# Prompt rows of eight experts fetched and turned together, the first expert's turn in two banks, the rotation of the first attention on GpSimd

## The reference

```
def apply_rope(x, cos, sin):
    x1, x2 = jnp.split(xf, 2, axis=-1)
    return jnp.concatenate([x1 * cos - x2 * sin, x2 * cos + x1 * sin], axis=-1)

def expert_choice_ffn(h, w_router, w_gate, w_up, w_down):      # 16 experts
    cap = EC_CAPACITY * T // N_EXPERTS                         # 128 sample rows, 16 prompt rows
    aff = jax.nn.softmax(jnp.einsum('btd,de->bte', h, w_router), axis=-1)
    gate, idx = lax.top_k(aff.swapaxes(1, 2), cap)
    xg = jax.vmap(lambda hb, ib: hb[ib])(h, idx)
    y = einsum(silu(xg @ w_gate) * (xg @ w_up), w_down) * gate
    return zeros.at[idx].add(y)                                # per group
```

## Time and profile before

| | us |
|---|---|
| median of three timed runs | 4399.0 (4393.88 to 4404.57) |
| profiled execution | 4391.62 |
| its span | 4389.8 |
| TensorE busy | 3666.0 (84%) |
| VectorE busy | 2445.7 (56%) |
| ScalarE busy | 1652.6 (38%) |
| GpSimd busy | 601.4 (14%) |
| mean granted clock of TensorE | 0.904 of full speed |

### The profile page before, as it was taken

One profiled execution on the slowest core, in us unless ns is written; L12 is line 12 of the kernel. 1 busy time (PEld: TensorE's weight loads), 2 busy tenths in 40 slices (PEclk: granted clock), 3 DMA queues, 4 the chain that ended last, 5 costly groups with the idle time before them and its releaser, 6 DMA issues. The chain is left out here.

```text
span 4389.8 us, 55873 instructions
## 1 busy us (share of the span) xinstructions
PE 3666.0 (84%) x22188; PEld 2687.1 (61%) x22188; DVE 2445.7 (56%) x3797; ACT 1652.6 (38%) x2480; POOL 601.4 (14%) x457
## 2 busy tenths in 40 slices
PE   3997869797839999999599978419996579999995
PEld 2994524343726666666499956319995446666663
DVE  3234341233477888887412454445555668888884
ACT  2114520000215555555211156524433145555653
POOL 2001110110100101000300000015651010101000
PEclk7998879898969999999699998759997789999997
DMA  4218521411536787777344120343325348777875
GB/s 157 89 60 280 170 72 72 162 53 50 174 141 237 282 294 277 271 278 281 109 118 114 63 92 13 108 145 80 99 55 197 134 160 293 283 270 273 291 283 193
DMA packets 363736, 743.38 MB, mean 169 GB/s; under 512 B 98888, under 2 KB 204247, under 8 KB 362376
## 3 DMA queue, kind: packets, MB, share of 16 engines
q1 hardware_dynamic: 343818, 683.00, 44.1%
q0 software_dynamic: 17040, 56.40, 5.1%
q10 hardware_dynamic: 2618, 0.40, 0.1%
HBM read 634.25 MB, written 106.10 MB: 169 GB/s over the span
## 5 line engine op out<-in xcount | busy, mean ns | idle before, releaser
L2023 DVE TENSOR_TENSOR moe_w_low<-ffn_w,moe_w_high 128x1024 fp32r<-128x1024 f32 x768 | 912.9, 1221 | 132.6 <-ACT moe_w_high L1956 116.5
L1956 ACT ACTIVATE moe_w_high<-ffn_w 128x1024 fp32r<-128x1024 f32 x768 | 785.7, 1055 | 436.1 <-DMA ffn_w<-moe_w_gate 144.0
L1886 PE MATMUL moe_small<-ffn_w,moe_xT 128*16 128x512 f32 x2048 | 238.3, 594 | 0.0
L1983 DVE TENSOR_SCALAR moe_xT<-moe_turn,keep_coef 128x128 f32<-128x128 f32 (+1 forms) x512 | 142.0, 344 | 116.7 <-PE moe_turn L1842 116.7
L1866 PE MATMUL moe_G<-moe_w_high,moe_xT_high 128*128 128x512 f32 x512 | 179.8, 433 | 16.1 <-issue 16.1
L297 PE MATMUL proj_mm<-proj_hT_low,proj_w_high 128*128 128x384 f32 x576 | 193.2, 335 | 0.0
L297 PE MATMUL proj_mm<-proj_hT_high,proj_w_low 128*128 128x384 f32 x576 | 193.1, 335 | 0.0
L297 PE MATMUL proj_mm<-proj_hT_high,proj_w_high 128*128 128x384 f32 x576 | 193.1, 335 | 0.0
L297 PE MATMUL proj_mm<-proj_w_high,proj_hT_low 128*128 128x416 f32 (+1 forms) x504 | 176.5, 350 | 0.0
L297 PE MATMUL proj_mm<-proj_w_high,proj_hT_high 128*128 128x416 f32 (+1 forms) x504 | 176.1, 349 | 0.0
L2547 PE MATMUL gdnc_a<-gdnc_T,gdnc_kg 128*128 128x64 f32 (+1 forms) x864 | 102.1, 267 | 88.3 <-ACT gdnc_T L2597 86.1
(11 more groups left out here) (450 smaller groups left out, 7555.5 us busy)
## 6 DMA issues: line engine op xcount, KB each, us to landing
ffn_w<-moe_w_gate SPq DMA_DIRECT2D x256, 512.0 KB, 7.0
ffn_w<-moe_w_up SPq DMA_DIRECT2D x256, 512.0 KB, 7.8
ffn_w<-moe_w_down SPq DMA_DIRECT2D x256, 512.0 KB, 5.9
attnrun_m_w<-w_ada SPq DMA_DIRECT2D x40, 1024.0 KB, 10.8
scratch_conv<-proj_zf POOLq DMA_DIRECT2D x24, 512.0 KB, 2.9
scratch_tm<-proj_tm SPq DMA_DIRECT2D x45, 208.0 KB, 2.0
proj_w_raw<-even_w_in SPq DMA_DIRECT2D x24, 384.0 KB, 3.9
scratch_spec<-filt_res SPq DMA_DIRECT2D x36, 256.0 KB, 2.2
```

Of the source, the lines that this page charges most:

```text
L1886: nc.tensor.matmul(out, stat, w, start=k == 0, stop=k == KD - 1, tile_position=(0, 32 * q)).then_inc(small_done, 1)
L1956: nc.scalar.activation(w_high[n % CUT_ROOM][:], raw_rows(wall, n), ACT.Copy).then_inc(w_up, 1)
L1983: ins = nc.vector.tensor_scalar(xT[e % 2][:, k, cols], turned(k)[:, cols], co[:, 0, k:k + 1], co[:, 1, k:k + 1], ALU.mult, ALU.add)
L2023: nc.vector.tensor_tensor(w_low[n % CUT_ROOM][:], raw_rows(wall, n), w_high[n % CUT_ROOM][:].bitcast(F32), ALU.subtract).then_inc(w_cut, 1)
```

## The change

Three things are changed. In `experts` the row numbers of the prompt slots go to memory and come back as one column of 128 for every eight experts; two indirect DMAs fetch all prompt rows of the layer, and four groups of four turns fill `xpT`, behind k = 0 to 3 of expert 0. An expert's sample rows are turned in two groups of four, behind k = 4 and 6 of the expert before; for expert 0 the second group goes to a bank of Y. `xT` has one buffer. The places of evictions, rounding and cutting move with them, and expert 0's small matmuls of k 0 to 3 all stand behind k = 5. The row of the prompt's gate is loaded as four pieces. In the attention of layer 0 the rotations of tiles 2 to 8 run on GpSimd, two ahead of each bias addition.

```diff
+        def rope(eng, ops, n):        # the body of VectorE's rope(n), on the engine given
...
             for n in order[:ready[0] + 1]:
                 if even and n < NT:
-                    rope(n)
+                    rope(dve, nc.vector, n)
...
-                if even and p % 4 == 1 and p // 4 in steady:
-                    rope(steady[p // 4])
...
+            turning = list(steady.values()) if even else []
+            if even:
+                pool.wait_ge(trig_in, 32)
-            for g in range(MG):
+            for g in range(max(MG, -(-len(turning) // 2))):
+                for n in turning[2 * g:2 * g + 2]:
+                    rope(pool, nc.gpsimd, n)
                 if g == 0:
                     pool.wait_ge(m_bias_in, 64)
...
-        fills = (range(0, 3), range(3, 6), range(6, KD))
+        NF = 2
+        def turned(k, e=1):
+            return (Y[:, 0, :] if e == 0 and k >= 4 else turn_bank)[:, (k % 4) * P:(k % 4 + 1) * P]
...
-            for c in range(2):
-                sp.dma_start(rowg[:, c, :], all_rows(io["mrow"][l, c, 5 * D:6 * D])).then_inc(row_in, 16)
+            sp.dma_start(rowg[:], all_rows(io["mrow"][l, 0, 5 * D:6 * D])).then_inc(row_in, 16)
+            for q in range(4):
+                src = io["mrow"][l, 1, 5 * D + 256 * q:5 * D + 256 * (q + 1)]
+                sp.dma_start(rowgp[32 * q:32 * (q + 1), :], all_rows(src, 32)).then_inc(row_in, 16)
...
+            def fetch_prompts():
+                pool.dma_start(io["prompt_rows"].rearrange("e r -> r e"), keep.slot_p[0:CAP_P, :].bitcast(F32),
+                               allow_slow_non_contiguous=True).then_inc(rows_out, 16)
+                pool.wait_ge(rows_out, 16)
+                pool.dma_start(rows_p[:].bitcast(F32), io["prompt_rows"].rearrange("(g j) r -> (j r) g", j=PG),
+                               allow_slow_non_contiguous=True).then_inc(rows_in, 16)
+                pool.wait_ge(rows_in, 16)
+                for g in range(E // PG):
+                    nc.gpsimd.indirect_dma_start(out=xgp[g][:], out_offset=None, in_=io["xn"],
+                                                 in_offset=bass.IndirectOffsetOnAxis(ap=rows_p[:, g:g + 1], axis=0)).then_inc(xgp_in, 16)
...
             fetch(0)
             fetch(1)
+            fetch_prompts()
...
-                for k in fills[i]:
-                    nc.tensor.transpose(turned(k)[:, 0:CAP_S], xg[e % 2][:, k * P:(k + 1) * P], keep.ident[:])
-                    mm = nc.tensor.transpose(turned(k)[:, CAP_S:SLOTS], xgp[e % 2][:, k * P:(k + 1) * P], keep.ident[0:CAP_P, 0:CAP_P])
+                for k in range(4 * i, 4 * i + 4):
+                    mm = nc.tensor.transpose(turned(k, e), xg[e % 2][:, k * P:(k + 1) * P], keep.ident[:])
+            def turn_prompts(n):
+                g, i = divmod(n, 2)
+                if n == 0:
+                    pe.wait_ge(xgp_in, 16 * (E // PG))
+                    pe.wait_ge(x_set, NF)
+                else:
+                    pe.wait_ge(xp_set, n)
+                for k in range(4 * i, 4 * i + 4):
+                    mm = nc.tensor.transpose(turned(k), xgp[g][:, k * P:(k + 1) * P], keep.ident[:])
+                mm.then_inc(xp_turned, 1)
...
-                    if e + 1 < E and k in (3, 5, 7):
-                        turn_tokens(e + 1, (k - 3) // 2)
-                    if k in (3, 5):
-                        small_rows(e, range(k - 3, k - 1), False)
+                    if e == 0 and k < 4:
+                        turn_prompts(k)
+                    if e + 1 < E and k in (4, 6):
+                        turn_tokens(e + 1, (k - 4) // 2)
+                    if k == 3 and e:
+                        small_rows(e, range(0, 2), False)
+                    if k == 5:
+                        small_rows(e, range(2 if e else 0, 4), False)
...
-                if (e, m, k) == (1, "u", 0):
+                if (e, m, k) == (1, "g", 1):
                     round_tokens(1)
-                if m == "d" and k == 3 and e + 2 < E:
+                if m == "d" and k == 1 and e + 2 < E:
                     round_tokens(e + 2)
...
-                if m == "g" and e + 1 < E and k in (5, 7):
-                    set_tokens(e + 1, (k - 5) // 2)
+                if e == 0 and m == "g" and 2 <= k < 6:
+                    set_prompts(k - 2)
+                if m == "g" and e + 1 < E and k == 6:
+                    set_tokens(e + 1, 0)
                 if (e, m, k) == (1, "g", 0):
-                    set_tokens(1, NF - 1)
-                if (e, m, k) == (1, "g", 1):
+                    set_tokens(1, 1)
+                if (e, m, k) == (1, "u", 1):
                     cut_tokens(1)
+                if m == "d" and k == 0 and e + 2 < E:
+                    set_tokens(e + 2, 1)
                 if m == "d" and k == 2 and e + 2 < E:
-                    set_tokens(e + 2, NF - 1)
-                if m == "d" and k == 3 and e + 2 < E:
                     cut_tokens(e + 2)
```

More of the change, by code:

```diff
@@ L784, in spread_sums @@
             mm.then_inc(spread_mm, 1)
+        def rope(eng, ops, n):
+            eng.wait_ge(tok_in[n], 16)
+            x = tok[:, n, 0:640].rearrange("p (h a d) -> p h a d", a=2, d=32)
+            q_out = tok[:, n, 0:512].rearrange("p (j s a d) -> p s j a d", s=2, a=2, d=32)
+            trig, c1, s1 = m["trig"], m["c1"], m["s1"]
+            if n:
+                eng.wait_ge(roped, n)
+            if n < NTS:
+                cos, sin = (trig[:, i, n:n + 1, :].unsqueeze(1).broadcast_to([P, 10, 2, 32]) for i in range(2))
+                ops.tensor_tensor(c1[:], x, cos, ALU.mult).then_inc(chain, 1)
+                ops.tensor_tensor(s1[:], x, sin, ALU.mult).then_inc(chain, 1)
+                eng.wait_ge(chain, 2 * n + 2)
+                for a, op in ((0, ALU.subtract), (1, ALU.add)):
+                    ops.tensor_tensor(x[:, 8:10, a, :], c1[:, 8:10, a, :], s1[:, 8:10, 1 - a, :], op)
+                    ins = ops.tensor_tensor(q_out[:, :, :, a, :], c1[:, 0:8, a, :].rearrange("p (s j) d -> p s j d", s=2),
+                                            s1[:, 0:8, 1 - a, :].rearrange("p (s j) d -> p s j d", s=2), op)
+            else:
+                ops.tensor_copy(c1[:], x).then_inc(chain, 1)
+                eng.wait_ge(chain, 2 * n + 1)
+                for a in range(2):
+                    ins = ops.tensor_copy(q_out[:, :, :, a, :], c1[:, 0:8, a, :].rearrange("p (s j) d -> p s j d", s=2))
+            ins.then_inc(roped, 1)
         @blk.tensor
@@ L875, in take_outputs @@
                 nc.vector.tensor_tensor(oT[:, g % 2], po[:], spread[:], ALU.mult).then_inc(o_done, 1)
[L877 to L898, removed]
             def take_keys(n):
@@ L1763, in experts @@
         xg = [s.sb(f"xg{i}", [P, D]) for i in range(2)]
-        xgp = [s.sb(f"xgp{i}", [CAP_P, D]) for i in range(2)]
-        xT = [s.sb(f"xT{i}", [P, KD, SLOTS]) for i in range(2)]
+        PG = P // CAP_P
+        rows_p = s.sb("rows_p", [P, E // PG], U32)
+        xgp = [s.sb(f"xgp{i}", [P, D]) for i in range(E // PG)]
+        xpT = s.sb("xpT", [P, KD, E // PG, P])
+        xT = s.sb("xT", [P, KD, CAP_S])
         xT_high, xT_low = ([s.sb(f"xT_{n}{i}", [P, KD, CAP_S], F32R) for i in range(2)] for n in ("high", "low"))
@@ L1774, in experts @@
         yp = [s.sb(f"yp{i}", [CAP_P, D]) for i in range(2)]
-        rowg = s.sb("rowg", [P, 2, D])
+        rowg = s.sb("rowg", [P, D])
+        rowgp = s.sb("rowgp", [P, 256])
         G, U, Y = (s.ps(n, [P, 2, BANK]) for n in "GUY")
@@ L1831, in turn_tokens @@
             def turn_tokens(e, i):
-                if i:
+                if e and i:
                     pe.wait_ge(x_set, NF * e + i)
-                else:
-                    pe.wait_ge(xg_in[e % 2], 32 * (e // 2 + 1))
+                elif i == 0:
+                    pe.wait_ge(xg_in[e % 2], 16 * (e // 2 + 1))
                     if e >= 2:
@@ L1870, in small_rows @@
             def small_rows(e, ks, down):
-                if not down and ks[0] == 0 and e >= 2:
-                    pe.wait_ge(yp_done, e - 1)
+                if not down and ks[0] == 0:
+                    pe.wait_ge(xp_set, 4)
+                    if e >= 2:
+                        pe.wait_ge(yp_done, e - 1)
                 if down and ks[0] == 0:
```

45 lines of the change are left out of this document (26 added, 19 removed).

## The result

The changed kernel takes 4346.0 us (median of 4 runs, 4344.0 to 4347.6) against 4396.4 (4 runs, 4393.1 to 4404.6): ratio 0.988, 95% interval 0.9865 to 0.990. The forecast was 4330, its range 4312 to 4358. It is faster, by 50 us and not by 69. The two profiled executions differ by 47.0 (spans 4389.8 and 4342.8).

The account below looks back on a forecast made before the run. TensorE's issue was taken as the bound. Gains and losses of 58 + 11 - 0.4 - 3.4 + 3.8 = 69 us gave 4322.6 off the profiled 4391.6, 4330 off the median 4399; range 4312 to 4358 with the nearer half of (a) and (b).

Parts of the forecast that it names:

- main case: Whole kernel: forecast of 4330 us off the median, spanning 4314 to 4343 by its bounds; chance 0.78 together with (d).
- part 1: Token turns of experts 1 to 15: 2.08 us saved a loop, 58 us over 28 loops; bounds 28 x 1.0 to 28 x 2.5.
- Part 2: First expert's start: TensorE starts 5.5 us earlier a layer, 11 us for two layers; bounds 8 to 13.
- Part 3: Prompt rows through GpSimd's queue: 4.7 us for each slot-number DMA, TensorE waits 0.2 us a layer; bounds nothing to 15.
- Part 4: Rest of loop 0: takes 41.2 us, 1.7 more than before, costing 3.4 us over two layers; bounds 0 to 8.
- Part 5: First attention's rotations moved from VectorE to GpSimd: TensorE waits of 3.8 us go; bounds 0 and 7.
- (a): Rival on the turns: 16-row turns only fill free slots or weights come late, 28 x 1.0 saved, 4360; chance 0.11.
- (d): Rival in attention: GpSimd late for the keys, 5 us lost replace 3.8 gained, 4339; chance 0.78 together with the main case.
- (b): Rival on prompt rows: each slot-number DMA takes 12.3 us, 2 x 15 us of waiting plus half-clock restarts, 4363; chance 0.08.
- (c): Rival in expert loops: VectorE blocked on turned tokens, later cuts slip, 76 us lost instead of 58 gained, 4464; chance 0.03.
- the 48 that would have refuted the forecast: Sign of being wrong in the expert loops: the period stays above 48 us an expert; 47.1 was forecast.
- this sign of being wrong: Sign at the first expert's start: prompt rows land later than 1310 us.

Follow-up runs that it names:

- a1: The changed kernel with rows_p allocated last, no longer amid the expert stage's tiles: 4335.4 us, ratio to the kernel before 0.986.
- b1: The kernel before with an unused 8-byte tile between xg and xgp, moving later expert-stage tiles by 32 bytes: 4417.8 us, ratio 1.0046.
- a5: a1 with both token-turn groups directly ahead of the small matmuls (k = 3 and 5, not 4 and 6) for experts 1 to 14: 4336.3 us.
- c1: a1 plus a5's turns, reordered loop 0 end, earlier small matmuls, later gate-row wait, earlier slot numbers, split prompt-fetch semaphores, early Silu load: 4310.6 us.

## Why the prediction was right in kind and 19 us off in size

- *The range*: the main case with its bounds was given as 4314 to 4343, and 4346 lies outside it. The result is inside 4312 to 4358 only because half of two rivals was added. The 4343 doesn't follow from the bounds either: part 1 at its own lower bound, 28 for 58, would by itself give 4360.
- *What bounds the kernel*: right. TensorE stands at 100 of 100 in the steady stretch, before and after; VectorE's slack and the weight transfers held, as costed.
- *Part 1, the mis-sized term*: 2.08 us a loop were forecast, 58 in all, and 1.39 x 28 = 39 came (the table's 37.7 also holds the last loops, which turn nothing and pay the shift). Of the missing 0.69, 0.51 (14 us) is the shifted tiles, shown by a1 and by b1 in the other kernel. The working priced what the diff issues and took for granted that the untouched pairs keep their 0.4545; the declaration of `rows_p` in the diff changed those. The other 0.18 (5 us): aligned, the period is 47.30. I priced the turns by their start-to-start cost and the entries by the entry alone, but the k step behind any interruption runs 0.03 or so slower as a whole (pairs of 0.46 to 0.47), and the old order had two k steps with no interruption ahead of them. That part is read from timelines; a5, which restores those two steps, gives back 0.12.
- *Part 2*: right. 5.3 and 5.7 us a layer against 5.5; first G matmul 13.8 us after the fetch against 14.
- *Part 3*: the value chosen failed, the bounds held. It was 4.7 us for each of the two DMAs; the write took 8.0 to 9.6 in all kernels that write 4-byte pieces, the reading back 2.5 to 2.9. The wait is 1.0 and 2.95 us, not 0.2. By the Trainium skill ("DMA: Bandwidth & Descriptors", "Anatomy of one DMA", some 2.0 us plus bytes) there would, as an estimate, have been no wait: the reading back is near that, the write isn't.
- *Part 4*: the new stall was called at some 5 us and is 5.41 and 4.83. Still the loop is longer than the 41.2 us forecast (the terms listed add up to 41.4): 43.2 and 44.1. Parts 3 and 4 together cost 9.3 where 3.8 were forecast; 4.0 of it are the waits for prompt rows, which leaves 5.3 for part 4 by itself, inside its bounds of 0 to 8. Of these 5.3 the stall is 1.4 more than before, weights called "about even" are 1.3, and some 3 (an estimate, half of 16.0 - 9.8 us) are time at clock 0.50, for which the working had 0.3 a layer. The matmuls themselves take some 0.5 less, with at most 1.1 for the 96 shifted pairs in it.
- *Part 5*: right in sign and in the waits that it named; it left out the clock. The rotation takes 5.1 us on GpSimd as forecast, and the three waits of 1.18, 1.24 and 1.37 us are gone. The stage is 7.3 shorter, just above the bound of 7: 3.8 of waits, and 6.8 us less at clock 0.50 (23.9 before, 17.1 after), worth some 3.4 as an estimate. In five of nine executions this second part did not come, or half of it did. The Trainium skill ("Perfetto Trace Analysis", "Optimizing Scalar/DVE Operations") says that such a move might not help, for the shared read port; read as a gain of 0, that did not hold here.
- *Rivals*: (a), half the turns' price at 4360, is 14 us from the result where the forecast is 16, but by luck: its mechanism, 16-row turns that fill free slots, did not hold, for aligned the turns save 1.89 a loop. (d), 4339, is nearest of all in number, and what it describes didn't occur: the attention gained. Of (b) the write is late, at 8.0 to 9.6 us and not 12.3, and the reading is early; the wait is 1 to 3 us and not 15. (c) did not occur.
- *Signs*: the turns, TensorE at 100 of 100, the first G matmul, the stall and the rotations came as called; VectorE's longest sum of the rotation now takes 0.42 us and not 2.26. The period, at 47.8, is short of the 48 that would have refuted the forecast. The wait for prompt rows was to be under 1 us and is 1.03 and 2.95. They were not to land later than 1310, which is 20.5 us behind the first fetch: TensorE goes on with them after 20.3 us in layer 0 and 21.6 in layer 1, so in one layer this sign of being wrong came.

## What to carry to other kernels

Read a diff's allocations as well as its instructions: where TensorE is the bound, a small tile between large ones shifts the operands behind it, and here 32 bytes cost 11 to 21 us by the medians. Small tiles go last. When a period misses its forecast, compare the median duration of instructions that did not change before looking for a wait. Look at the granted clock of a stage beside its waits: here a wait also cost time at half clock behind it, and executions of the same stage differed by it. When work is moved to one engine's earlier slot, check what its queue then puts ahead of the piece that another engine stands for; a change of order at the end of loop 0 was worth about as much as the layout (11.8 us by the medians, against 10.6).

## What the hardware showed that I had not expected

- Operands in SBUF: fp32r matmuls of 128x512 with one operand's tile 32 or 64 bytes past a multiple of 128 take a median of 394 to 400 ns for 389 in the lines of U and Y (0.466 to 0.469 against 0.4545 us a pair start to start, clock 1.00), the stationary and the moving one alike. Why is open.
- The 16-row small matmuls did not change: 16 of them took 1.83 to 1.85 us, with their stationary tile at either place.
- 256 pieces of 4 bytes on GpSimd's queue: 8.0 to 9.6 us to land as a write, 2.5 to 2.9 as a read; 16 pieces of 64 bytes still 4.6 to 5.4 behind two fetches. A fetch of 128 rows with such a write directly behind it reached TensorE after 8.4 and 9.3 us (c1, one case in each layer), and after 5.0 to 6.3 with the other fetch between, in the two layers of nine kernels. The link is likely; no run changes the order alone.
- Granted clock: two levels only, and executions of the same stage differ in when it falls. The 64 matmuls of a modulation group took 3.63 us at 1.00 and 6.38 at 0.56.
